# Sample state updates of a gated linear attention on row groups of 32, with two masked copies of the keys

## The reference, cut to what matters

```python
def gla_chunk(S, q, k, v, g):
    b = jnp.cumsum(g, axis=1)
    o_inter = jnp.einsum('bthd,bhde->bthe', q * jnp.exp(b), S)
    ...
    o_intra = jnp.einsum('bhts,bshe->bthe', A, v)
    b_last = b[:, -1]
    k_dec = k * jnp.exp(b_last[:, None] - b)
    S_new = jnp.exp(b_last)[..., None] * S + jnp.einsum('bshd,bshe->bhde', k_dec, v)
    return S_new, o_inter + o_intra
```

## Time and profile before

| | |
|---|---|
| runs | 1605.76, 1605.52, 1599.19 us; median 1605.52 |
| profiled execution | 1606.0 us, of which the trace spans 1604.2 us |
| granted TensorE clock, mean over the span | 0.981 of full speed |
| busy share of the span | PE 97%, PEld 95%, DVE 68%, ACT 29%, POOL 32% |
| the stage of the change | about 248 to 322 us, four heads |

### The profile page before, as it was taken

The page is one execution under the profiler, slowest core; times in us unless marked ns, Lnnn a source line. Parts: engine busy times, 40 slices in busy tenths (PEclk is TensorE's granted clock), DMA queues, the critical chain, the costliest instruction groups (busy, mean ns, idle before and its releaser), DMA issues.

```text
span 1604.2 us, 26209 instructions
## 1 busy us (share of the span) xinstructions
PE 1548.5 (97%) x10292; PEld 1527.5 (95%) x10292; DVE 1085.5 (68%) x1313; ACT 461.0 (29%) x717; POOL 511.7 (32%) x221
## 2 busy tenths in 40 slices
PE   6999999999999999999998999998999999999994
PEld 5999998899999999999998999998999999999994
DVE  6656665854976667777767545457976677777667
ACT  4345554443222112112215111115211121222214
POOL 4422221143333333333332333332333333333221
PEclk9999998999999999999999999998999999999997
DMA  5221115222222222222222222222122222222201
GB/s 208 66 66 53 54 53 205 112 70 68 70 75 66 78 70 74 78 78 77 67 65 67 77 79 76 69 66 68 53 79 79 65 78 78 78 75 69 66 33 70
DMA packets 34862, 123.59 MB, mean 77 GB/s; under 512 B 3920, under 2 KB 6864, under 8 KB 33648
## 3 DMA queue, kind: packets, MB, share of 16 engines
q1 hardware_dynamic: 31872, 108.37, 21.5%
q10 hardware_dynamic: 2928, 14.35, 2.4%
HBM read 114.48 MB, written 8.22 MB: 76 GB/s over the span
## 4 chain that ended last, share of the span: by engine, by line
PE 45%; issue 35%; POOL 12%; DVE 4%; DVEq 2%; ACT 1%; DMA 0%; POOLq 0%; SPq 0%; ACTq 0%
PE ps L404 28%; POOL wl L348 12%; PE ps L420 9%; PE ps L587 2%; PE ps L487 2%; PE ps L689 1%; PE ps L539 1%; DVE sq L726 1%; DVE y L963 1%; DVEq L724 1%; PE ps L501 1%; DVEq L1000 0%; POOL ol L363 0%; DMA x<-x_t 0%; DVE y L959 0%
## 5 line engine op out<-in xcount | busy, mean ns | idle before, releaser
L348 POOL TENSOR_TENSOR wl<-raw,wh 128x1024 fp32r<-128x1024 f32 x195 | 485.7, 2493 | 979.0 <-ACT wh L1165 979.0
L404 PE MATMUL ps<-xh,wh 128*128 128x328 f32 (+5 forms) x2176 | 506.8, 314 | 18.9 <-DVE xl L710 16.0
L404 PE MATMUL ps<-xl,wh 128*128 128x328 f32 (+5 forms) x2176 | 503.4, 313 | 0.0
L404 PE MATMUL ps<-xh,wl 128*128 128x328 f32 (+5 forms) x2176 | 503.1, 313 | 0.0
L404 PEld LDWEIGHTS ps<-xh,wh 128*128 128x128 f32 x2176 | 389.3, 191 | 21.8 <-issue 13.8
L404 PEld LDWEIGHTS ps<-xl,wh 128*128 128x128 f32 x2176 | 390.5, 190 | 0.0
L404 PEld LDWEIGHTS ps<-xh,wl 128*128 128x128 f32 x2176 | 389.8, 190 | 0.0
L1165 ACT ACTIVATE wh<-raw 128x1024 fp32r<-128x1024 f32 x196 | 206.4, 1055 | 242.5 <-PE ps L404 227.7
L963 DVE SCALAR_TENSOR_TENSOR y<-zp,par,y 128x660 f32<-128x660 f32 (+1 forms) x192 | 182.0, 948 | 29.4 <-issue 27.0
L1309 ACT COPY zl<-zp 128x18 f32 (+1 forms) x88 | 18.3, 208 | 627.7 <-DVE y L963 627.7
L420 PE MATMUL ps<-gh,wh 128*128 128x322 f32 (+1 forms) x800 | 184.4, 312 | 5.4 <-issue 5.4
(11 more groups left out here) (154 smaller groups left out, 1181.1 us busy)
## 6 DMA issues: line engine op xcount, KB each, us to landing
raw<-w_units SPq DMA_DIRECT2D x196, 512.0 KB, 3.5
s<-states ACTq DMA_DIRECT2D x4, 1024.0 KB, 5.6
state_sample<-snew ACTq DMA_DIRECT2D x4, 1024.0 KB, 4.2
x<-x_t SPq DMA_DIRECT2D x8, 328.0 KB, 5.7
x<-x_t ACTq DMA_DIRECT2D x1, 2624.0 KB, 13.4
y_t<-x SPq DMA_DIRECT2D x6, 320.0 KB, 2.4
ffn_last<-zl ACTq DMA_DIRECT2D x2, 396.0 KB, 2.9
zc<-ffn_cache ACTq DMA_DIRECT2D x1, 704.0 KB, 4.1
```

The costliest lines, as they stand in the source:

```text
L348: pool.tensor_tensor(wl[:, j, :, :], raw[:, j, :, :], wh[:, j, :, :].bitcast(F32), ALU.subtract).then_inc(sem["lo_done"], 1)
L404: mm = pe.matmul(ps[:, p, c:c + z - a], w[:, ring, k, :], v[:, k, a:z], start=(k == 0 and w is wh and v is hi), stop=(k == KT - 1 and w is ...
```

## The change

Rows are taken in groups of 32, which hold two sequences each. So two masked copies of the keys are enough, one with the even and one with the odd sequences, and ScalarE writes two in place of four. TensorE issues the tail's update first, then waits for the slots of both `("U", h, 1)` and `("U", h, 2)`, then issues sequences 0, 2, 4, 6 (rows 0, 32, 64, 96 on) and then 1, 3, 5, 7. The plan of the slots puts the tail in front of `("U", h, 1)`. `filled` of `("U", h, 1)` comes with sequence 3, the sixth of the eight, and that of `("U", h, 2)` with sequence 7.

```diff
-        s.straight(("U", h, 0), ("U", h, 1), ("U", h, "tail"), ("U", h, 2))
+        s.straight(("U", h, 0), ("U", h, "tail"), ("U", h, 1), ("U", h, 2))
...
-    kd = sb("kd", [P, 9, P], offset=b_at)
+    kd = sb("kd", [P, 7, P], offset=b_at)
...
-            for j in (1, 2):
-                if j == 2:
-                    open_slot(("U", h, "tail"))
-                    mm, p = update(h, "tail", 0, kd[0:16, 4, :], v_tok[0:16, 4, vs])
-                    mm.then_inc(filled[p], 1)
-                open_slot(("U", h, j))
-                for n in range(4):
-                    s = 4 * (j - 1) + n
-                    rows = slice(64 * (s // 4), 64 * (s // 4) + 64)
-                    mm, p = update(h, j, n, kd[rows, 5 + s % 4, :], v_tok[rows, 5, vs])
-                mm.then_inc(filled[p], 1)
+            open_slot(("U", h, "tail"))
+            mm, p = update(h, "tail", 0, kd[0:16, 4, :], v_tok[0:16, 4, vs])
+            mm.then_inc(filled[p], 1)
+            open_slot(("U", h, 1))
+            open_slot(("U", h, 2))
+            for odd in range(2):
+                for t in range(SEQS // 2):
+
+                    s = 2 * t + odd
+                    rows = slice(32 * t, 32 * t + 32)
+                    mm, p = update(h, 1 + s // 4, s % 4, kd[rows, 5 + odd, :], v_tok[rows, 5, vs])
+                    if odd and t % 2:
+                        mm.then_inc(filled[p], 1)
...
-            for j in range(4):
+            for j in range(2):
                 last = act.activation(kd[:, 5 + j, :], ps[:, p, 5 * P:6 * P], ACT.Copy,
-                                      scale=par[:, C_FOURTH + j:C_FOURTH + j + 1])
+                                      scale=par[:, C_EVEN + j:C_EVEN + j + 1])
...
-    for j in range(4):
-        par[:, C_FOURTH + j] = np.arange(P) // SLEN % 4 == j
+    for j in range(2):
+        par[:, C_EVEN + j] = np.arange(P) // SLEN % 2 == j
```

More of the change, by code:

```diff
@@ L74 @@
 C_SCW = 52
-C_FOURTH = 76
+C_EVEN = 76
 C_EPS, C_HALF_EPS = 80, 81
```

## The result

The changed kernel is slower. Over 14 runs of each its median is 1616.66 us (1604.6 to 1621.37) against 1601.6 us (1596.67 to 1612.48); the estimated ratio is 1.0076, 95% interval 1.0052 to 1.0100, or 12 us (the two medians lie 15 us apart, the two means 11). The mean granted clock of the 14 runs is 0.9731 (0.967 to 0.979).

The account below looks back on a forecast made before the run. VectorE was taken to bound heads 2 and 3, TensorE head 1 alone, with head 0 almost level. The terms +0.38 - 1.11 + 0.39 + 0.39 = +0.05 us on 1606.0 gave 1606.1 us, range 1599 to 1611.

Parts of the forecast that it names:

- TensorE is not what sets the end in heads 2 and 3: Heads 2 and 3: TensorE's updates lie beside VectorE's work, whose release comes 0.11 us before the next step.
- The overlap: Tail and sample updates: four updates on four row groups run as one, so 4.46 us becomes 1.6.
- The bound without overlap: Tail and sample updates: if the matmuls do not overlap, the stretch takes 3.8 us; chance 0.25, time 1606.7.
- 0.33 us at every change of form: TensorE's weight loads: a gap of 0.33 us comes ahead of each change of matmul form.
- The swapped wait, directly: Transposes or first outputs wait for the tail: +0.38 us in head 0, -1.11 in head 1, +0.39 in heads 2 and 3.
- The added wait for both output slots, and ScalarE's copies: Ahead of the first sample update, and 8 fewer masked copies on ScalarE: both costed at nothing.
- the sum: Effects on heads 0 to 3 added up: +0.05 us, or +0.7 without overlap.
- the granted clock falls more often: Rival: more TensorE idle time brings more falls; two cost 10.2 us, giving 1616.3. Chance 0.06 for two or more.
- the window from 305 to 308: Trace before: thin updates, loads in 1.85 of 3 us, clock 1.00; taken as evidence against more clock falls.
- My own sign of being wrong: Heads 2 or 3: a 3-us window with a clock near 0.5 would show the prediction wrong.
- The base: Whole kernel: the profiled execution of 1606.0 us, with the median of the runs 0.5 us below it.
- regained falls: Rival: a shift in time moves the clock falls away, -6.9 us, 1599.2 us; chance 0.08.

Follow-up runs that it names:

- after_fill: The changed kernel plus three 128x512 fp32 matmuls per head, read by nothing, right behind the eight sample updates; ratio to the kernel before 1.0008.
- one_group: The changed kernel with all eight updates of a head on rows 0 to 31, so without overlap; ratio to the kernel before 1.0072.
- after_again: The changed kernel repeated unaltered, on another chip than the first comparison; ratio to the kernel before 1.0080.
- before_cut: The kernel before with six of each head's eight sample updates left out, still on 64 rows; ratio to the kernel before 1.0037.
- one_group_slots: The changed kernel with all eight updates on rows 0 to 31 and the plan's order of before; ratio to the kernel before 1.0072.
- swap_only: The kernel before, 64 rows, with the tail issued first and placed ahead of sequences 0 to 3 in the plan; ratio to the kernel before 1.0030.
- after_slots: The changed kernel with the plan's order of before, sequences 0 to 3 ahead of the tail; ratio to the kernel before 1.0027.
- slots_fill2: The changed kernel with the plan's order of before and two 128x512 fp32 filler matmuls ahead of the head norm; ratio to the kernel before 0.9975.

## Why the prediction was wrong

**TensorE is not what sets the end in heads 2 and 3: right.** The updates left the chain, and nothing of 2.9 us a head came off.

**The overlap: right.** "Below, four updates on four row groups run as one" gave 1.6 us for the stretch. Measured from the tail's first load to the next matmul that may follow (after_fill) it is 1.16 + 0.33 = 1.5 us. The sum is closer than its terms: the tail costs less than its 0.62, since the gap behind it is gone, and the eight updates more than 0.96. The bound without overlap, 3.8, was a little low: one_group has 3.75 + 0.33 = 4.1. And 0.33 us at every change of form holds for the updates, but not for the 16-row part within the outputs, where the loads pause for 0.13 us at most.

**The swapped wait, directly: right to a tenth.** Head 0's output starts at 256.54 where 248.79 is its first update; before it was 256.06 and 248.70, so +0.39 for the forecast +0.38. From head 3's first update to its first output it is 304.82 to 313.09, 8.27 us, for 303.38 to 311.26, 7.88: +0.39 as forecast. In head 2 it is 9.20 for 8.48, +0.72: the swap's 0.39, and 0.3 because the transposes ran at half clock. Head 1's stretch, 270.77 to 278.38, is 7.61 for 10.07 us, but the clock differs in it. The trace of after_again has head 1's prompt updates at half clock, as the trace before had:

```profile
273.75 1.16 PEld L539 LDWEIGHTS ps<-v_tok,kd 16*128 16x128 f32 x18 [0.33 <-issue]
278.95 0.53 PEld L589 LDWEIGHTS ps<-AT,v_tok 128*128 128x128 f32 x4
```

From the first load behind them to the output it takes 5.20 us there, for 6.31 before (271.34 to 277.65): -1.11, as forecast.

**The added wait for both output slots, and ScalarE's copies: right.** The updates follow the tail without a gap, and VectorE waits for `filled` nowhere.

**The clock: wrong, and all of the result.** The step that failed is in the sum: it has no term for the granted clock, and takes TensorE's longer idle time as free. Its only place was the rival "the granted clock falls more often", with a chance of 0.06 for two or more falls. Measured were a mean clock of 0.9731 for 0.9833 and 12 us. I had the rival's mechanism and nearly its price, 10.2 us from two more falls. That the price fits so well is in part luck: the trace does have two more falls, but they are of other lengths and cost 8.5 us in the stage, and other executions differ. I set the rival aside with one row: the window from 305 to 308 with the thin updates at a clock of 1.00. That window was not evidence against it. In the trace before, the clock fell some us behind the thin updates, in the outputs (at 261 in head 0, at 316 in head 3; the latter is the 0.61 of the window from 317), so this head spoke for the rival. My own sign of being wrong then came: the changed kernel has a clock of 0.50 in the window from 293 to 296, in head 2. The sum took the gain in TensorE's work as harmless where it is hidden. It is not: before_cut shows 0.4% lost from leaving work out. And I had no term for the form. one_group_slots, as busy as the kernel before, loses 0.7% with 32 rows. The rule of the Trainium skill that I quoted ("TensorE: Matmul & The Clock Gate", Part 1), the low clock as default that activity lifts, agrees with much of these traces and not with all: in the trace before, the clock is 0.50 from 1590 us on, where TensorE does nothing more, but 1.00 in the first 8 us, where it does nothing yet, and it falls at 261 after 5 us of dense outputs. It should have had the larger chance all the same.

**The base: a small miss.** The profiled execution of 1606.0 lay above the median of 14 runs, 1601.6, by 4 us. Runs of the kernel before differ by the clock as well: of the 35 beside after_again, the fastest, 1594.08 us, has 0.990 and the slowest, 1611.68, has 0.977. The "regained falls" rival described this, and not the change.

What stays open: why the swapped wait, worth 0.1% directly, moves the clock so far that the ratio moves by 0.3% (swap_only) to 0.5% (changed against after_slots); how the shares of idle time and of the form add up, since one_group_slots, with the form and without the swap or the idle time, is as slow as the changed kernel with all three, while after_slots, with the form and the idle time, loses only 0.3%; and whether the filling helps by the time that it covers or by the work that it adds.

## What to carry to other kernels

Where TensorE waits for another engine anyway, making its matmuls shorter or narrower bought next to nothing here, and it can lower the granted clock of the dense matmuls behind them: read the clock in the windows after each thin stretch before pricing such an edit at nothing. Price a saving on a hidden TensorE stretch from both sides, with the cost of a fall (here 5.1 us for 10 us at half clock) as the bad end and a real chance. If the smaller form is wanted, dense matmuls that nothing reads can hold the clock in the gap, as in after_fill and slots_fill2; keep them shorter than the slack.

## What the runs showed of the hardware

fp32 matmuls on distinct groups of 32 rows overlap: 18 loads in 1.16 us against 3.75 us on one group, where each takes 0.21 us, as a 128-row update does (8 loads in 1.60 us). It does not need four different groups in a row, since pairs on the same rows took 1.29 us. The Trainium skill ("TensorE: Matmul & The Clock Gate", Part 3) has matmuls on different tiles of the array run at the same time, and gives 3.07 times for four row tiles; the trace agrees, with 3.75/1.16 = 3.2. The 16-row tail and the 32-row updates follow each other without the 0.33 us gap that stands between 128, 64 and 16 rows in the updates before. And a mean granted clock that is lower by 0.013 came with 17.6 us between two runs of one kernel: most of the run-to-run spread, and of the differences between these kernels, goes with the clock (1.29 us for each 0.001, by the 99 runs).
